# Attention: high and low query parts turned as one operand, four maxima in one narrow turn

## The chip, the cores and the metric

The kernel runs on one core of one Trainium2 chip. The metric is the device time of one launch in microseconds (us). The kernel before takes 1848.46 us, the median of three runs (1845.34 to 1849.5).

## What is computed

Two layers of a hybrid backbone over 1024 latent tokens and 128 context tokens. Each layer projects the tokens, runs a pooling mixer, softmax attention and a gated DeltaNet in parallel, gates the three and projects out. The change is in the attention alone:

```python
def one_block(qblk):
    s = jnp.einsum('bqkgd,bskd->bkgqs', qblk, k, preferred_element_type=jnp.float32) * scale
    p = jax.nn.softmax(s, axis=-1).astype(v.dtype)
    return jnp.einsum('bkgqs,bskd->bqkgd', p, v)
```

There are 8 query heads and 2 key/value heads of dimension 64. Latent queries see 1024 latent keys, 128 cached keys and their own softmax; context queries see the 128 context keys.

## The kernel before

Everything is float32 in effect. A score needs more precision than one pass of the fast format (fp32r) gives, so each operand is split into a high part (its fp32r rounding) and a low part (the rest), and a score is the sum high x high + high x low + low x high.

**How the attention is tiled.** Work goes by "pairs" p = 0 to 8. Pair 0 is the context. Pairs 1 to 8 are each one block of 512 latent tokens of one key head and one pair of its query heads. Each pair has two "asks" (p, i), i = 0 and 1, of four blocks of 128 queries, 18 asks in a layer. A pair has 9 steps (pair 0 has one), one for each tile of 128 keys: 73 steps in a layer. `BASE[p]` is the first step of pair p: 1, 10, 19, 28, 37, 46, 55, 64 for p = 1 to 8. In step n TensorE makes the scores of both query halves (L1642 and L1643, bank 0 and bank 1 of PSUM), ScalarE takes the exponential (L1492), GpSimd adds up the exponentials (L1426) and TensorE multiplies them with the values (L1652). `scores(n)` needs the exponentials of step n-1, since the two banks are used again.

**How a query gets ready.** GpSimd's `split` (L1400) writes the high part twice side by side into `qhh` (two casts, L1409) and the low part into `ql` (L1412); for the first four asks ScalarE makes the high part (`query_high`, L1501). TensorE turns the four blocks of `qhh` (item "hi", four transposes, L1559) into PSUM bank 7 and ScalarE copies them into `QH` (L1468), so that rows 0 to 63 and rows 64 to 127 of `QH` both hold the high part. Item "max" multiplies a block with all keys (L1606) and VectorE reduces it to one maximum for each query (L1679), written into column 64 of `ql`. Item "lo" turns the four blocks of `ql` with that column (four transposes of 65 columns, L1588), and ScalarE copies the 65 rows into `QL` (L1468). Row 64 of `KO` is -1, so the maximum is subtracted within the second score product.

**How keys get ready.** ScalarE and GpSimd make high and low parts in `khl` (L1498, L1431) while TensorE runs the scan of the DeltaNet. `key_turn` turns them between scan steps (L1569). ScalarE copies both into `KH` (`keys_turned`, L1507) and later the high part from `KH` into `KO` (`keys_copied`, L1512).

**What sets the order.** Each engine's instructions run in the written order. `attention_slots` (L1243) writes it: in slot n TensorE does scores(n+1), then the slot's items, then the values of step n; ScalarE does the exponentials of step n+1, then the copies of the slot's items; VectorE does the slot's items. The items of pair p with b = `BASE[p]` lie at:

```python
slots[b - 8].append(("hi", p, 1))
slots[b - 6].append(("lo", p, 0))
slots[b - 2].append(("lo", p, 1))
if p >= 3:
    slots[b - 12].append(("hi", p, 0))
```

The DeltaNet's outputs are turned as items "o" in slots 8 to 16 (L1625). Items "hi", "lo", "sum" and "o" all use PSUM bank 7, so each turn waits until the copy of the turn before it is done (`turn_start`, L1548). Asks of pairs 0 and 1 and "hi" (2, 0) come before the steps, in the list `first` (L1245). The scores of a pair's first step wait for the copy of its "lo" (p, 1) (L1637). GpSimd's adds and splits are in one order too (L1449 to L1463).

## Time and profile before

| | |
|---|---|
| median of the runs | 1848.46 us |
| the profiled execution | 1844.25 us, its span on the core 1842.6 us |
| busy TensorE / VectorE / ScalarE / GpSimd | 91% / 53% / 34% / 50% of the span |
| granted clock of TensorE, mean | 0.964 of full speed |
| attention steps, layer 1 and layer 2 | 577.5 to 803 us and 1496 to 1722 us |

PE is TensorE's matmul, PEld its weight load, DVE VectorE, ACT ScalarE, POOL GpSimd, SP the queue that issues transfers. In a timeline row the first number is the start in us from the start of the span, the second how long the row took; "x4" means four instructions merged, and then the second number runs from the first start to the last end. Behind it, in brackets, stands how long the engine was idle before it and which instruction ended that wait.

### The profile page before, as it was taken

Reading aid. Unit: us, or ns where it says so; the run is one execution under the profiler, and the core shown is the slowest. Engines: PE = TensorE matmul, PEld = TensorE weight load, DVE = VectorE, ACT = ScalarE, POOL = GpSimd, SP = SyncE. Lnnn points to the kernel's source line nnn. Section 1 sums busy time; section 2 is a strip of 40 time slices with the busy share of each in tenths; the row PEclk is TensorE's granted clock in tenths of the full one; section 3 lists DMA queues with packets and bytes.
Section 4 is the critical chain, followed back from the end, with each engine's and each line's share of the span. In section 5 each row is a group of like instructions: output and inputs, shape, how many; then the busy total and the mean of one; then the engine's idle time right before and its main releaser. Section 6 shows DMA issues by size and latency. Waiting matters only on the chain. (4 is left out here: it accounts for less than half of the span.)

```text
span 1842.6 us, 40839 instructions
## 1 busy us (share of the span) xinstructions
PE 1678.3 (91%) x17404; PEld 1367.6 (74%) x17404; DVE 978.3 (53%) x1476; ACT 623.5 (34%) x1238; POOL 928.4 (50%) x858
## 2 busy tenths in 40 slices
PE   4999999989988899979849999999899888999798
PEld 3898999979975445548728989999799754455586
DVE  2646316377736785552126563164677467955611
ACT  4322310144443444451133223111444424444511
POOL 1003395089943878832210033950899448788332
PEclk8999999999988999989969999999999999999899
DMA  9301113110000020032283011121100000200222
GB/s 338 120 14 59 61 58 93 59 37 21 4 11 13 6 58 17 12 115 92 82 308 124 31 59 61 58 85 64 39 22 4 12 13 6 64 12 12 115 91 92
DMA packets 71247, 117.22 MB, mean 64 GB/s; under 512 B 10129, under 2 KB 42129, under 8 KB 71057
## 3 DMA queue, kind: packets, MB, share of 16 engines
q1 hardware_dynamic: 70128, 114.18, 18.3%
q8 instruction: 140, 2.29, 0.5%
q10 hardware_dynamic: 928, 0.34, 0.1%
q14 instruction: 51, 0.41, 0.1%
HBM read 95.03 MB, written 19.47 MB: 62 GB/s over the span
## 5 line engine op out<-in xcount | busy, mean ns | idle before, releaser
L1426 POOL TENSOR_TENSOR attn_accp<-attn_accp,attn_pr 128x1024 f32<-128x1024 f32 x112 | 268.7, 2399 | 49.3 <-ACT attn_pr L1492 43.3
L93 PE MATMUL ps<-h_hi,in_w_hi 128*128 128x384 f32 (+1 forms) x816 | 275.9, 338 | 5.0 <-DVE h_lo L456 4.9
L94 PE MATMUL ps<-h_lo,in_w_hi 128*128 128x384 f32 (+1 forms) x816 | 274.6, 336 | 0.0
L95 PE MATMUL ps<-h_hi,in_w_lo 128*128 128x384 f32 (+1 forms) x816 | 274.4, 336 | 0.0
L1679 DVE TENSOR_REDUCE attn_ql<-ps 128x1 f32<-128x1152 f32 x128 | 172.9, 1356 | 119.9 <-PE ps L1606 119.5
L1492 ACT ACTIVATE attn_pr<-ps 128x512 f32<-128x512 f32 x292 | 158.6, 595 | 189.9 <-PE ps L1643 189.1
L93 PEld LDWEIGHTS ps<-h_hi,in_w_hi 128*128 128x128 f32 (+1 forms) x816 | 150.1, 184 | 13.1 <-issue 6.7
L94 PEld LDWEIGHTS ps<-h_lo,in_w_hi 128*128 128x128 f32 (+1 forms) x816 | 150.2, 184 | 3.9
L95 PEld LDWEIGHTS ps<-h_hi,in_w_lo 128*128 128x128 f32 (+1 forms) x816 | 150.1, 184 | 3.9
L1642 PEld LDWEIGHTS ps<-attn_QH,attn_KH 128*128 128x128 f32 x292 | 55.0, 188 | 126.3 <-issue 53.5
L1652 PE MATMUL ps<-attn_pr,z 128*64 128x512 f32 x520 | 141.3, 622 | 0.0
L908 POOL TENSOR_TENSOR delta_ML<-delta_EK,local 128x256 f32<-128x256 f32 x180 | 130.5, 746 | 14.9 <-PE ps L945 14.2
L1642 PE MATMUL ps<-attn_QH,attn_KH 128*128 128x512 f32 x292 | 131.2, 449 | 2.5 <-ACT attn_pr L1492 2.5
L945 PE MATMUL ps<-delta_TR,delta_ML 64*64 64x64 f32 x2880 | 112.8, 224 | 16.1 <-POOL delta_ML L908 10.1
L93 PE MATMUL ps<-in_w_hi,h_hi 128*128 128x256 f32 x432 | 124.6, 288 | 0.0
L288 POOL TENSOR_TENSOR in_scratch<-zz 128x1175 f32<-128x1175 f32 x4 | 9.3, 2332 | 228.0 <-ACT zz L716 228.0
L94 PE MATMUL ps<-in_w_lo,h_hi 128*128 128x256 f32 x432 | 122.9, 284 | 0.0
L95 PE MATMUL ps<-in_w_hi,h_lo 128*128 128x256 f32 x432 | 122.8, 284 | 0.0
L945 PEld LDWEIGHTS ps<-delta_TR,delta_ML 64*64 64x64 f32 x2880 | 98.9, 138 | 23.9 <-issue 11.7
L1643 PE MATMUL ps<-attn_QL,attn_KO 65*128 65x512 f32 x292 | 115.9, 397 | 0.0
L352 DVE CAST in_w_hi<-in_w 128x2048 fp32r<-128x2048 f32 (+1 forms) x24 | 31.1, 1295 | 152.7 <-DMA in_w<-in_w_in 152.7
L1606 PE MATMUL ps<-attn_KH,attn_QH 128*128 128x384 f32 x384 | 94.8, 358 | 14.3 <-DVE attn_ql L1679 13.3
(248 smaller groups left out, 3604.3 us busy)
## 6 DMA issues: line engine op xcount, KB each, us to landing
in_w<-in_w_in SPq DMA_DIRECT2D x22, 1024.0 KB, 6.0
zz<-in_w_mod SPq DMA_DIRECT2D x8, 2048.0 KB, 13.3
gates<-in_gate SPq DMA_DIRECT2D x48, 192.0 KB, 1.9
attn_gt<-gates SPq DMA_DIRECT2D x34, 256.0 KB, 2.6
z<-in_w_mod SPq DMA_DIRECT2D x4, 2048.0 KB, 10.2
out_w<-in_w_out SPq DMA_DIRECT2D x16, 512.0 KB, 7.0
delta_GB<-gc_rows SPq DMA_DIRECT2D x36, 128.0 KB, 2.9
z<-out_y SPq DMA_DIRECT2D x9, 512.0 KB, 10.7
```

Of the source, the lines that this page charges most:

```text
L93: nc.tensor.matmul(out, a_hi(i), b_hi(i), start=(i == 0), stop=False)
L94: nc.tensor.matmul(out, a_hi(i), b_lo(i), start=False, stop=False)
L95: last = nc.tensor.matmul(out, a_lo(i), b_hi(i), start=False, stop=(i == n - 1))
L908: nc.gpsimd.tensor_tensor(pairs(ML[d][:, i % 2]), EA[d][:, j % 3, :, 0], level_mask(i, d), ALU.mult).then_inc(ml_done, 1)
L945: last = nc.tensor.matmul(heads(bank, off)[rows(c), h, :], lhs(rows(c), h), rhs(rows(c), h), start=True, stop=True)
L1426: nc.gpsimd.tensor_tensor(acc, a, pr[:, n % 4], ALU.add).then_inc(pool_added, 1)
L1492: nc.scalar.activation(pr[:, n % 4, e], ps[:, e, :], ACT.Exp, scale=HD ** -0.5).then_inc(p_done, 1)
L1606: last = nc.tensor.matmul(ps[:, bank + c, 0:GRP], QH[:, p % 3, blk // 2, col:col + P], KH[:, g, GRP * c:GRP * c + GRP], start=True, stop=True)
L1642: nc.tensor.matmul(ps[:, e, :], KH[:, g, ks], QH[:, p % 3, e, :], start=True, stop=False)
L1643: nc.tensor.matmul(ps[:, e, :], KO[0:HD + 1, g, ks], QL[0:HD + 1, p % 2, e, :], start=False, stop=True).then_inc(st_done, 1)
L1652: nc.tensor.matmul(ps[HD * e:HD * e + HD, 2 + p % 2, :], values(p, kt, e), pr[:, n % 4, e], start=(kt == 0), stop=(kt == STEPS_OF[p] - 1)) ...
L1679: nc.vector.tensor_reduce(ql[:, a % 4, blk, HD:HD + 1], ps[:, bank:bank + 3, 0:GRP], AX_XY, ALU.max).then_inc(mx_read, 1)
```

## The change

The roles of the halves are exchanged. The query operand now has the high part in columns 0 to 63 and the low part in columns 64 to 127 (`qhl`), so one turn of four blocks brings both. The keys are laid out to fit: `KH` holds the high part in both row halves, `KO` the low part and four rows of -1 below it. The first score product is key high x (query high + query low), the second key low x query high, minus the maximum. ScalarE copies a turned "hi" item twice: 128 rows into `QH`, and rows 0 to 63 again into `QM`. The maxima of an ask's four blocks stand in four columns of `mx`; the "lo" item is one transpose of 4 columns, which gives 4 rows of 128. ScalarE spreads them with four small copies into rows 64 to 67 of `QM`, one for each block, each with a per-partition scale that is a unit column of the identity, so that for a block one row has its maximum and three rows are zero. For the keys, ScalarE copies the low half into `KO` and the high half into rows 64 to 127 of `KH`, and GpSimd copies that to rows 0 to 63 (`keys_doubled`). GpSimd's split has one cast in place of two, and `query_high` one activation in place of two. The copies from `KH` to `KO` are gone.

```diff
-    QL, rc = sb("QL", [P, 2, 2, QB], F32R), sb("rc", [P, 2, QB])
+    rc = sb("rc", [P, 2, QB])
+    sb("gap", [P, 1408])
-    QH = sb("QH", [P, 3, 2, QB], F32R)
-    qhh, ql = sb("qhh", [P, 4, 4, P]), sb("ql", [P, 4, 4, HD + 2])
+    QH, QM = sb("QH", [P, 3, 2, QB], F32R), sb("QM", [P, 3, 2, QB], F32R)
+    qhl, mx = sb("qhl", [P, 4, 4, P]), sb("mx", [P, 4, 4])
...
@@ GpSimd: split
-            for e in range(2 if n >= 4 else 0):
-                nc.gpsimd.tensor_copy(blocks(qhh[:, n % 4, :, HD * e:HD * e + HD], p).bitcast(F32R), q)
+            hi, lo = (blocks(qhl[:, n % 4, :, HD * e:HD * e + HD], p) for e in range(2))
             if n >= 4:
+                nc.gpsimd.tensor_copy(hi.bitcast(F32R), q)
                 pool.drain()
-            nc.gpsimd.tensor_tensor(blocks(ql[:, n % 4, :, 0:HD], p), q, blocks(qhh[:, n % 4, :, 0:HD], p),
-                                    ALU.subtract).then_inc(q_split, 1)
+            nc.gpsimd.tensor_tensor(lo, q, hi, ALU.subtract).then_inc(q_split, 1)
...
+        def keys_doubled(j):
+            pool.wait_ge(k_act, j + 1)
+            cols = slice(256 * j, 256 * j + 256)
+            pool.drain()
+            nc.gpsimd.tensor_copy(KH[0:HD, :, cols], KH[HD:P, :, cols]).then_inc(k_both, 1)
+            pool.drain()
...
         split(0, 0)
+        keys_doubled(0)
+        keys_doubled(1)
         split(0, 1)
         key_low(4)
+        keys_doubled(2)
         split(1, 0)
+        keys_doubled(3)
         split(1, 1)
-        pool.drain()
-        nc.gpsimd.memset(KO[HD:HD + 1].bitcast(F32), -1.0).then_inc(ones_done, 1)
+        keys_doubled(4)
+        nc.gpsimd.memset(KO[HD:HD + 4].bitcast(F32), -1.0).then_inc(ones_done, 1)
...
@@ ScalarE: evict
-                copied(item, query_columns(QH[:, p % 3], p, i), turned_columns(slice(0, P), p))
+                is_turned(act, *item)
+                nc.scalar.activation(query_columns(QH[:, p % 3], p, i), turned_columns(slice(0, P), p), ACT.Copy)
+                nc.scalar.activation(query_columns(QM[0:HD, p % 3], p, i), turned_columns(slice(0, HD), p),
+                                     ACT.Copy).then_inc(turn_copied, 1)
...
-                r = slice(0, HD + 1)
-                copied(item, query_columns(QL[r, p % 2], p, i), turned_columns(r, p))
+                is_turned(act, *item)
+                for b in range(4):
+                    e, c = (i, P * b) if p == 0 else (b // 2, 256 * i + P * (b % 2))
+                    last = nc.scalar.activation(QM[HD:HD + 4, p % 3, e, c:c + P], ps[0:4, 7, 0:P], ACT.Copy, scale=m["ident"][0:4, b:b + 1])
+                last.then_inc(turn_copied, 1)
...
@@ ScalarE: keys_turned; keys_copied and its calls are removed
-            nc.scalar.activation(KH[:, :, 256 * j:256 * j + 256], ps[:, K_BANKS[j], :].rearrange("p (g c) -> p g c", g=2),
-                                 ACT.Copy).then_inc(k_act, 1)
+            lo, hi = (ps[HD * e:HD * e + HD, K_BANKS[j], :].rearrange("p (g c) -> p g c", g=2) for e in range(2))
+            cols = slice(256 * j, 256 * j + 256)
+            nc.scalar.activation(KO[0:HD, :, cols], lo, ACT.Copy)
+            nc.scalar.activation(KH[HD:P, :, cols], hi, ACT.Copy).then_inc(k_act, 1)
...
@@ TensorE: the "lo" item, the first maxima and the scores
-                for blk in range(4):
-                    last = nc.tensor.transpose(ps[0:HD + 1, 7, P * blk:P * blk + P], ql[:, n % 4, blk, 0:HD + 1], m["ident"])
-                last.then_inc(turned, 1)
+                nc.tensor.transpose(ps[0:4, 7, 0:P], mx[:, n % 4, :], m["ident"]).then_inc(turned, 1)
...
                     pe.wait_ge(o_out, NT)
+                    pe.wait_ge(k_both, len(K_BANKS))
...
-                nc.tensor.matmul(ps[:, e, :], KO[0:HD + 1, g, ks], QL[0:HD + 1, p % 2, e, :],
+                nc.tensor.matmul(ps[:, e, :], KO[0:HD + 4, g, ks], QM[0:HD + 4, p % 3, e, :],
...
@@ VectorE: maximum
-                nc.vector.tensor_reduce(ql[:, a % 4, :, HD], ps[:, bank, :].rearrange("p (h c) -> p h c", c=P), AX_X,
+                nc.vector.tensor_reduce(mx[:, a % 4, :], ps[:, bank, :].rearrange("p (h c) -> p h c", c=P), AX_X,
```

## Rows read from the trace of the kernel before

**Rows 1.** Windows: busy us (xinstructions) by engine, clock, DMA, first layer's steps
```profile
577.50:803.00 225.50, 211.26 (x910) 112.05 (x910) 148.51 (x129) 103.87 (x192) 176.72 (x102) 0.99 0.07 19
```

**Rows 2.** Groups by line, shapes apart: busy us, mean ns | idle before
```profile
L1588 PE MATMUL ps<-masks,attn_ql 128*65 128x128 f32 x144 | 23.4, 288 | 3.4 <-DVE attn_ql L1679 3.1 <-ACT attn_QL L1468 0.3
...
L1468 ACT ACTIVATE attn_QL<-ps 65x512 fp32r<-65x512 f32 x36 | 21.4, 594 | 43.7 <-PE ps L1588 43.7
...
L714 ACT ACTIVATE zz<-ps 128x384 f32<-128x384 f32 x32 | 14.8, 491 | 67.0 <-PE ps L95 67.0
...
L1144 ACT ACTIVATE pbr<-ps,cols 128x384 f32<-128x384 f32 x12 | 6.5, 576 | 4.3 <-PE ps L1059 2.6 <-PE ps L1062 1.7
...
L716 ACT ACTIVATE zz<-ps 128x128 f32<-128x128 f32 x16 | 4.4, 275 | 0.0
...
L1409 POOL CAST attn_qhh<-z 128x256 fp32r<-128x256 f32 x56 | 21.9, 417 | 10.2 <-PE ps L1588 10.2
```

**Rows 3.** Timeline, a "lo" turn, the values behind it, the next exponentials
```profile
596.14 0.60 PE L1588 MATMUL ps<-masks,attn_ql 128*65 128x128 f32 x4
596.67 1.08 PE L1652 MATMUL ps<-attn_pr,z 128*64 128x512 f32 x4
...
598.45 1.09 ACT L1492 ACTIVATE attn_pr<-ps 128x512 f32<-128x512 f32 x2 [1.07 <-PE ps L1643]
```

**Rows 4.** Timeline around slot 17, the first scores of pair 3
```profile
641.01 1.09 ACT L1492 ACTIVATE attn_pr<-ps 128x512 f32<-128x512 f32 x2 [1.19 <-PE ps L1643]
...
642.43 0.59 ACT L1468 ACTIVATE attn_QL<-ps 65x512 fp32r<-65x512 f32 x1 [0.34 <-PE ps L1588]
...
643.33 0.50 PE L1642 MATMUL ps<-attn_QH,attn_KH 128*128 128x512 f32 x1
```

**Rows 5.** Timeline around slot 62, the first scores of pair 8
```profile
776.37 0.59 ACT L1468 ACTIVATE attn_QL<-ps 65x512 fp32r<-65x512 f32 x1
...
777.21 0.50 PE L1642 MATMUL ps<-attn_QH,attn_KH 128*128 128x512 f32 x1
```

**Rows 6.** Timeline in slot 8, a "lo" turn with an "o" turn behind it
```profile
609.47 0.59 ACT L1468 ACTIVATE attn_QL<-ps 65x512 fp32r<-65x512 f32 x1 [0.36 <-PE ps L1588]
...
610.11 0.44 PE L1625 MATMUL ps<-masks,of 128*128 128x128 f32 x2 [0.68 <-ACT attn_QL L1468]
```

**Rows 7.** Timeline of TensorE, "hi" (3, 0) in slot 7
```profile
605.68 0.63 PE L1559 MATMUL ps<-masks,attn_qhh 128*128 128x128 f32 x4 [1.44 <-POOL attn_ql L1412]
```

**Rows 8.** Timeline of the stage ahead of the steps, first layer
```profile
570.63 4.12 DVE L1679 TENSOR_REDUCE attn_ql<-ps 128x1 f32<-128x1152 f32 x3 [0.39 <-PE ps L1606]
...
575.55 0.59 ACT L1468 ACTIVATE attn_QL<-ps 65x512 fp32r<-65x512 f32 x1 [2.10 <-PE ps L1588]
...
576.30 0.60 PE L1559 MATMUL ps<-masks,attn_qhh 128*128 128x128 f32 x4
...
578.16 0.47 PE L1642 MATMUL ps<-attn_QH,attn_KH 128*128 128x512 f32 x1 [1.26 <-ACT attn_pr L1492]
```

**Rows 9.** Timeline of the last key turn, in the scan, and the first maxima
```profile
544.10 0.60 ACT L1509 ACTIVATE attn_KH<-ps 128x512 fp32r<-128x512 f32 x1 [0.60 <-PE ps L1569]
...
544.80 0.30 ACT L1498 ACTIVATE attn_khl<-z 128x128 fp32r<-128x128 f32 x1
...
545.17 0.45 POOL L1431 TENSOR_TENSOR attn_khl<-attn_ck,attn_khl 128x128 f32<-128x128 f32 x1 [1.46 <-ACT attn_khl L1498]
...
546.09 0.66 PE L1569 MATMUL ps<-masks,attn_khl 128*128 128x128 f32 x4 [1.41 <-POOL attn_khl L1431]
...
560.69 1.08 PE L1601 MATMUL ps<-attn_KH,attn_QH 128*128 128x128 f32 x8 [0.62 <-DVE of L1215]
```

**Rows 10.** Timeline of TensorE, from a wide stationary operand to one of 16 columns
```profile
136.91 0.34 PE L95 MATMUL ps<-h_hi,in_w_lo 128*128 128x384 f32 x1
137.08 0.34 PE L93 MATMUL ps<-h_hi,in_w_hi 128*16 128x384 f32 x1
```

**Rows 11.** Timeline of TensorE, the values of step 0
```profile
582.58 1.98 PE L1652 MATMUL ps<-attn_pr,z 128*64 128x512 f32 x4
```

More of the change, by code:

```diff
@@ L1291, in attention @@
     khl = sb("khl", [P, KT_CTX + 1, NKV, P])
-    QH = sb("QH", [P, 3, 2, QB], F32R)
-    qhh, ql = sb("qhh", [P, 4, 4, P]), sb("ql", [P, 4, 4, HD + 2])
+    QH, QM = sb("QH", [P, 3, 2, QB], F32R), sb("QM", [P, 3, 2, QB], F32R)
+    qhl, mx = sb("qhl", [P, 4, 4, P]), sb("mx", [P, 4, 4])
     onc = sb("onc", [P, 1])
     cache_in, on_in, kv_out = sem("cache_in"), sem("on_in"), sem("kv_out")
-    ones_done, k_high, k_split, k_turned, k_act, k_copied, q_high = (
-        sem(n) for n in ("ones_done", "k_high", "k_split", "k_turned", "k_act", "k_copied", "q_high"))
+    ones_done, k_high, k_split, k_turned, k_act, k_both, q_high = (
+        sem(n) for n in ("ones_done", "k_high", "k_split", "k_turned", "k_act", "k_both", "q_high"))
     turned, turn_copied = sem("turned"), sem("turn_copied")
@@ L1497, in key_high @@
             for ks, k in keys_of(j):
-                last = nc.scalar.activation(khl[:, ks, :, 0:HD].bitcast(F32R), k, ACT.Copy)
+                last = nc.scalar.activation(khl[:, ks, :, HD:P].bitcast(F32R), k, ACT.Copy)
             last.then_inc(k_high, 1)
@@ L1502, in query_high @@
             n = ASKS.index((p, i))
-            for e in range(2):
-                last = nc.scalar.activation(blocks(qhh[:, n % 4, :, HD * e:HD * e + HD], p).bitcast(F32R), queries(p, i), ACT.Copy)
-            last.then_inc(q_high, 1)
+            nc.scalar.activation(blocks(qhl[:, n % 4, :, 0:HD], p).bitcast(F32R), queries(p, i), ACT.Copy).then_inc(q_high, 1)
         def keys_turned(j):
             act.wait_ge(k_turned, j + 1)
-            nc.scalar.activation(KH[:, :, 256 * j:256 * j + 256], ps[:, K_BANKS[j], :].rearrange("p (g c) -> p g c", g=2),
-                                 ACT.Copy).then_inc(k_act, 1)
-        def keys_copied(j):
-            act.wait_ge(k_act, j + 1)
-            nc.scalar.activation(KO[0:HD, :, 256 * j:256 * j + 256], KH[0:HD, :, 256 * j:256 * j + 256],
-                                 ACT.Copy).then_inc(k_copied, 1)
+            lo, hi = (ps[HD * e:HD * e + HD, K_BANKS[j], :].rearrange("p (g c) -> p g c", g=2) for e in range(2))
+            cols = slice(256 * j, 256 * j + 256)
+            nc.scalar.activation(KO[0:HD, :, cols], lo, ACT.Copy)
+            nc.scalar.activation(KH[HD:P, :, cols], hi, ACT.Copy).then_inc(k_act, 1)
         for j in range(4):
@@ L1530, in scalar @@
         evict(("hi", 0, 1))
-        for j in range(3):
-            keys_copied(j)
         evict(("hi", 1, 0))
-        for j in range(3, 5):
-            keys_copied(j)
         act.wait_ge(on_in, 32)
@@ L1558, in query_turn @@
         for blk in range(4):
-            last = nc.tensor.transpose(ps[:, 7, P * blk:P * blk + P], qhh[:, n % 4, blk, :], m["ident"])
+            last = nc.tensor.transpose(ps[:, 7, P * blk:P * blk + P], qhl[:, n % 4, blk, :], m["ident"])
         last.then_inc(turned, 1)
@@ L1634, in scores @@
                 pe.wait_ge(ones_done, 1)
-                pe.wait_ge(k_copied, len(K_BANKS))
             if kt == 0:
```

4 lines of the change are left out of this document (2 added, 2 removed).

## The prediction

> **What bounds the kernel now.** I read the page first. Its chain of work that ended last lies in the output projection and says nothing of the attention, so I went to the windows. In the first layer's steps (225.5 us) TensorE is busy for 211.26 us at a clock of 0.99, GpSimd for 176.72, VectorE for 148.51, ScalarE for 103.87 [rows 1]. The second layer's window reads alike. So the steps are bound by TensorE, and TensorE's own list of waits says where not. Then the timelines, slot by slot. The reader is to see three things there: the transposes that the change removes are short and overlap [rows 2, 3], the copy behind a "lo" turn has room in most slots but none in some [rows 4 to 6], and ahead of the steps TensorE is not the bound, VectorE's reductions and ScalarE's copies are [rows 8].
>
> **What a turn costs.** Four transposes take 0.60 us from the first start to the last end [rows 3] and one about 0.27 (the mean of 0.288 over 144 [rows 2] holds some at half the clock). So one follows another by (0.60 - 0.27) / 3 = 0.11 us, and three fewer free 0.33 us of TensorE. There are 36 "lo" turns in the two layers: at most 36 x 0.33 = 11.9 us. That is the whole prize, and each turn has to be asked who waits for what behind it. I take the one transpose of 4 columns at the time of one of 65: a stationary operand of 16 columns follows one of 128 after 0.17 us, the spacing of its neighbours, with no gap [rows 10].
>
> **What spreading costs.** One copy of 65x512 took 0.59 us [rows 2]. Four copies of 4x128 from PSUM with a scale read from SBUF replace it. The trace has a 128x128 copy from PSUM at 0.275, and the price of such a scale by 128x384 with and without: 0.576 - 0.491 = 0.085 [rows 2]. That makes 0.36 for one. Two exponentials of 0.595 take 1.09 together [rows 4], so each starts 0.10 before the end of the one ahead; the four take 0.36 + 3 x 0.26 = about 1.16 us. The low bound is 3 x 0.20 + 0.27 = 0.87, by the spacing of the two small key casts (the one at 544.80 came 0.20 after its neighbour) and no price for the scale [rows 9, 2]. The high bound is no overlap, 4 x 0.365 = 1.46. I take 1.16, since the shape and the scale are both priced by near rows.
>
> For this term the Trainium skill (ScalarE: Activation LUTs, section What ACT_TABLE_LOAD costs) gives 186 ns plus 0.833 ns a column, 93 ns more for a pointer operand, and an overlap of 93 ns: an estimate of 0.386 + 3 x 0.293 = 1.27 us for the four. By that figure the sum below would end some 1.9 us later (0.105 us at nine places in each layer). It agrees with the rows within a tenth and speaks against the change, since most of a small copy is its fixed part.
>
> **The "lo" turns of a layer, all 18.**
> - (4, 0) to (8, 0), in slots b - 6: nothing waits for the copy soon. The turn would end at 596.14 + 0.27 = 596.41 and the next exponentials move from 598.45 to 598.12 [rows 3]; 1.16 fits. Each frees 0.33: 5 x -0.33 = -1.65.
> - (3, 1) to (7, 1), in slots b - 2: the pair's first scores wait for the copy. Before, it started at 642.43 and was over 0.3 before the scores at 643.33 [rows 4]. Now the turn ends 0.33 earlier, ScalarE is just free of the exponentials (641.01 + 1.09 = 642.10), and the copies end at 642.10 + 1.16 = 643.26; with 0.06 for the signal the scores start at 643.32. TensorE would be ready at 643.00. The gain is eaten whole: 5 x 0.
> - (8, 1), slot 62, has no "max" item ahead of it, so ScalarE, not the turn, sets the start: 776.37 as before, end 777.53, scores at 777.59 in place of 777.21 [rows 5]: +0.38.
> - (2, 1) and (3, 0), slots 8 and 13: an "o" turn waits in the same slot for the bank. The copy starts at 609.47 - 0.33 = 609.14 and ends at 610.30, the "o" turn comes at 610.35 in place of 610.11 [rows 6]: 2 x +0.24 = +0.48.
> - (2, 0), slot 4: "hi" (3, 0) waits 1.44 us for GpSimd three slots later [rows 7] and swallows it: 0.
> - (0, 0): ahead of the steps, at half the clock, it held up the next maximum's product, and VectorE stood idle for 0.39 [rows 8]. I take most of that: -0.35.
> - (0, 1) and (1, 0): under VectorE's reductions, three in 4.12 us without a gap [rows 8]: 0.
> - (1, 1): next point.
>
> **The start of the steps.** Before, VectorE ends at 570.63 + 4.12 = 574.75, the "lo" (1, 1) turn follows, its copy starts at 575.55, "hi" (2, 0) is turned at 576.30 and copied, and only then come the exponentials of step 0, for which the scores of step 1 wait till 578.16 [rows 8]. Now the copies run from 575.22 to 576.38, the turn comes at 576.44 (+0.14), and its second copy puts another 0.49 (the spacing of two copies of 512 columns [rows 4]) ahead of the exponentials: +0.63.
>
> **The second copy of a "hi" item** adds 0.49 us on ScalarE 36 times. In most slots ScalarE has 1 us to spare. In slots 11 and 16 an "o" turn waits for it as the one of slot 8 does for its "lo" [rows 6]: 2 x +0.49 = +0.98.
>
> **GpSimd's split** loses one cast (0.42 by its mean [rows 2], and a little of it overlaps its neighbour, so I take 0.35), and "hi" (3, 0) comes that much earlier [rows 7]: -0.35. Elsewhere the splits are early.
>
> **The keys.** ScalarE's copy of each turned key tile becomes two, 0.49 more. The first three hide beside scan steps. The fourth, at 544.10, is in front of the casts of the last key tile, GpSimd's 0.9 us after them and the turn that TensorE already waits 1.41 us for, with scan steps queued behind it [rows 9]: 546.09 becomes 546.58, +0.49. The five doublings on GpSimd are of 64x512; by the cast of 128x256 at about 0.4 they take some 0.65 each. The maxima first need `k_both` at 560.69 [rows 9]. Even if all five only began when the last key turn is over, at 546.6 + 0.7, and the last two splits and the memset lay between them, they would be done with microseconds in hand: hidden. The five copies to `KO` that go, and the halved `query_high`, were beside scan steps: 0. Were the cover gone, the five would cost 3.3 us a layer.
>
> **The sum for a layer:** -1.65 + 0.38 + 0.48 - 0.35 + 0.63 + 0.98 - 0.35 + 0.49 = +0.61; two layers +1.2 us. Against the profiled execution (1844.25 us, span 1842.6) that is 1845.5; that execution lies 4.2 below the median, and on the median of 1848.46 the forecast is 1849.7. With four copies in 0.87 us the places read: slots b - 2 five times -0.30, slot 62 +0.09, slots 8 and 13 -0.05 each, start +0.34; sum -2.05 a layer, -4.1 in all. With 1.46 us: five times +0.29, +0.68, twice +0.54, start +0.93; +3.26 a layer, +6.5 in all.
>
> **The rivals.** A difference under 0.2% (3.7 us) cannot be told from none in this kernel.
> - Small copies are quicker than I price them, so that TensorE's gain comes through at the pair starts: 1848.5 - 4.1 = 1844.4. For it: only 4 of 128 partitions are written, and the small casts lay 0.20 apart [rows 9]. Against it: the scale's 0.085 [rows 2]. It decides from about 0.9 us for the four. Chance 0.23.
> - The other side, ScalarE becomes the bound at the pair starts: the four don't overlap. 1848.5 + 6.5 = 1855.0. Place: slots b - 2; it decides from about 1.35 us for the four. For it: the scale is one more read at each start. Against it: the exponentials overlap by 0.10 [rows 4]. Chance 0.15.
> - A narrow turn makes TensorE drain. From the last transpose's start to the half-width values there are 596.67 - (596.14 + 3 x 0.11) = 0.20 us where 0.11 is the spacing [rows 3]: 0.1 us for the change of shape. Once more at 13 turns a layer (five freed, five at pair starts, slots 8 and 13, (1, 1)) it would be +2.6 us: 1852.3. Against it rows 10. Chance 0.05. The Trainium skill (TensorEngine Tiling (Array Packing), Key Properties) says that changing the tiling mode drains TensorE; whether 4 columns are another mode no row here shows.
> - The clock falls longer at the start. Behind the wait of 1.26 us [rows 8] the values of step 0 took 1.98 us [rows 11], where later ones take 1.08 [rows 3]: half the clock. With 0.6 us more waiting ahead of them another step's worth might go, about 1.4 us a layer, 1852.5. Chance 0.07.
> - That the copies hide wholly and all 11.9 us come is excluded by rows 5 and 6.
>
> **How the numbers follow.** The forecast has 0.47, and its own range is 1846.5 to 1852.5. The range of 1843.5 to 1856 takes in the first two rivals and about 1 us beyond them. Faster: nearly all of the first rival and a tail, 0.25. Slower: most of the second, part of the two small ones and a tail, 0.26. The rest, 0.49, is no difference.
>
> **What would show it.** Each "lo" item is one transpose of about 0.27 us with the values 0.20 us behind its start; four ScalarE copies in 1.16 us; the first scores of pairs 3 to 7 wait about 0.3 us for them; "o" turns in slots 8, 11, 13, 16 wait 1.1 to 1.3 us in place of 0.7; the last key turn waits 0.5 us longer; `k_both` ends nobody's wait. The prediction is wrong if the four copies take under 0.9 or over 1.35 us, if TensorE has a gap around the narrow turn, or if VectorE's and GpSimd's order shifts so that TensorE's waits for them grow or go.

## The result, and the profile after

The changed kernel takes 1864.64 us, the median of five runs (1859.85 to 1868.04). The kernel before, run beside it, takes 1847.26 (1845.34 to 1849.5, five runs). The ratio is 1.0092, with a 95% interval of 1.007 to 1.0114. So the change costs about 17 us, where 1.2 were forecast. The profiled execution took 1868.04 us, its span is 1866.3. From the two pages, the busy times (before, then after) and the granted clock after in 40 slices:

```profile
PE 1678.3 (91%) x17404; PEld 1367.6 (74%) x17404; DVE 978.3 (53%) x1476; ACT 623.5 (34%) x1238; POOL 928.4 (50%) x858
```

```profile
PE 1691.6 (91%) x17296; PEld 1368.1 (73%) x17296; DVE 977.0 (52%) x1476; ACT 657.8 (35%) x1374; POOL 923.9 (50%) x840
...
PEclk8999999999987999989869999999999879999899
```

The engines' shares hardly differ from those of before. But TensorE carries 108 instructions fewer and is busy 13.3 us longer, and its mean clock is 0.947, where it was 0.964. So the time has to be looked for by stage. I cut each layer at three instructions of TensorE that both kernels have: the first product of the DeltaNet scan, the first "max" product, and the first product that sums the exponentials (item "sum"), up to the last of these. The windows of the kernel before, first layer (us, then busy us by PE, PEld, DVE, ACT and POOL, the granted clock, the DMA share, GB/s):

```profile
535.40:560.70 25.30, 22.54 (x597) 19.35 (x597) 12.25 (x43) 11.90 (x28) 8.77 (x12) 0.90 0.07 18
560.70:586.40 25.70, 19.34 (x79) 13.43 (x79) 14.67 (x12) 5.95 (x11) 6.90 (x7) 0.80 0.07 22
586.40:802.10 215.70, 204.02 (x889) 108.39 (x889) 145.80 (x127) 100.67 (x185) 176.72 (x102) 1.00 0.07 20
```

The same windows of the changed kernel, first layer; the second layer's read alike, with clocks of 0.85, 0.59 and 0.98:

```profile
532.60:560.60 28.00, 23.98 (x596) 20.55 (x597) 12.35 (x43) 13.23 (x28) 11.77 (x17) 0.84 0.07 16
560.60:589.80 29.20, 22.27 (x67) 14.59 (x67) 14.50 (x12) 8.68 (x24) 6.26 (x5) 0.59 0.06 19
589.80:807.40 217.60, 202.53 (x847) 104.05 (x847) 145.53 (x127) 114.11 (x240) 172.38 (x90) 0.98 0.07 20
```

| us, layer 1 and layer 2 | before | after | difference |
|---|---|---|---|
| scan | 25.3, 23.2 | 28.0, 27.5 | +2.7, +4.3 |
| start: first maximum to first sum | 25.7, 25.1 | 29.2, 29.2 | +3.5, +4.1 |
| steps: first to last sum | 215.7, 215.8 | 217.6, 217.7 | +1.9, +1.9 |

The six differences add up to 18.4 us. The two profiled executions lie further apart than the medians (spans of 1866.3 and 1842.6 us, 23.7 apart, against 17.4), and the other 5.3 us lie in stages that no kernel here changes. The longest of these, between the steps of layer 1 and the scan of layer 2, takes 654.4 us before and 660.9 after, and 654.2 to 661.2 over all the profiles of this document. So a single stage of one profile proves little, and the ratios decide.

The clock is the first thing to see. In the start of layer 1 TensorE carries 12 instructions fewer and is busy for 2.93 us longer (22.27 against 19.34), at a granted clock of 0.59 in place of 0.80. In the steps it is not so: TensorE is busy 1.49 us less and the stage is still 1.9 longer.

**The keys.** Timelines of TensorE and ScalarE in the scan of the changed kernel, first layer:

```profile
540.67 0.65 PE L1577 MATMUL ps<-masks,attn_khl 128*128 128x128 f32 x4
...
541.85 0.59 ACT L1526 ACTIVATE attn_KO<-ps 64x512 fp32r<-64x512 f32 x1
542.45 0.59 ACT L1527 ACTIVATE attn_KH<-ps 64x512 fp32r<-64x512 f32 x1
543.07 0.31 ACT L1515 ACTIVATE attn_khl<-attn_ck 128x128 fp32r<-128x128 f32 x1
...
544.57 1.03 PE L1577 MATMUL ps<-masks,attn_khl 128*128 128x128 f32 x4 [2.63 <-POOL attn_khl L1431]
545.53 0.69 PE L1079 MATMUL ps<-delta_S,zz 64*64 64x64 f32 x8
...
548.45 0.45 PE L1079 MATMUL ps<-delta_S,zz 64*64 64x64 f32 x8
```

These answer to [rows 9]. The wait ahead of the last key turn is 2.63 us, where it was 1.41. Behind it the turn takes 1.03 us (0.66 before) and eight scan products 0.69 us, where the same eight take 0.45 three microseconds later: TensorE runs at 1.2 GHz (granted clock 0.50) from the end of the wait to about 548.1, some 3.4 us. Before, the turn and the products behind it ran at 2.4 GHz.

**The start of the steps**, which answers to [rows 8]:

```profile
574.95 0.27 PE L1595 MATMUL ps<-masks,attn_mx 128*4 128x128 f32 x1 [1.81 <-DVE attn_mx L1685]
575.25 1.10 ACT L1493 ACTIVATE attn_QM<-ps,masks 4x128 fp32r<-4x128 f32 x4 [1.56 <-PE ps L1595]
575.96 0.63 PE L1648 MATMUL ps<-attn_QH,attn_KH 128*128 128x512 f32 x1
576.81 1.05 PE L1567 MATMUL ps<-masks,attn_qhl 128*128 128x128 f32 x4
...
579.60 0.76 PE L1648 MATMUL ps<-attn_QH,attn_KH 128*128 128x512 f32 x1 [1.74 <-ACT attn_pr L1509]
...
585.44 1.98 PE L1658 MATMUL ps<-attn_pr,z 128*64 128x512 f32 x4
```

**Slot 7**, which answers to [rows 7]:

```profile
608.77 0.63 PE L1567 MATMUL ps<-masks,attn_qhl 128*128 128x128 f32 x4 [1.42 <-POOL attn_qhl L1413]
609.33 1.79 PE L1658 MATMUL ps<-attn_pr,z 128*64 128x512 f32 x4
...
613.47 0.27 PE L1595 MATMUL ps<-masks,attn_mx 128*4 128x128 f32 x1
614.94 0.44 PE L1632 MATMUL ps<-masks,of 128*128 128x128 f32 x2 [1.20 <-ACT attn_QM L1493]
```

The wait is 1.42 us, as it was 1.44 [rows 7], and yet the values behind it take 1.79 us. In the kernel before they took 1.08:

```profile
606.24 1.08 PE L1652 MATMUL ps<-attn_pr,z 128*64 128x512 f32 x4
...
608.83 0.60 PE L1588 MATMUL ps<-masks,attn_ql 128*65 128x128 f32 x4
```

From the values to the "lo" turn it is 613.47 - 609.33 = 4.14 us, before 608.83 - 606.24 = 2.59: 1.55 us lost to the clock alone, and 1.55 in the second layer too.

That the wait is as long as before hides that both its sides came earlier. GpSimd's casts, before and after:

```profile
603.94 0.73 POOL L1409 CAST attn_qhh<-z 128x256 fp32r<-128x256 f32 x2
```

```profile
607.37 0.39 POOL L1411 CAST attn_qhl<-z 128x256 fp32r<-128x256 f32 x1
```

The low part starts 0.87 us behind the first cast before (604.81) and 0.53 after (607.90). TensorE is there sooner by the 0.33 of the narrow turn in slot 4. From the first sum to this turn it is 608.77 - 589.78 = 18.99 us, before 605.68 - 586.36 = 19.32.

The changed kernel's steps have a second stretch of 3.4 us at half the clock in each layer, at 684.3 us in the first, behind a wait for VectorE. After, and the same place before:

```profile
684.70 1.30 PE L1613 MATMUL ps<-attn_KH,attn_QH 128*128 128x384 f32 x3 [1.63 <-DVE attn_mx L1685]
```

```profile
679.59 0.77 PE L1606 MATMUL ps<-attn_KH,attn_QH 128*128 128x384 f32 x3 [1.32 <-DVE attn_ql L1679]
```

From there to the next scores it is 688.41 - 684.70 = 3.71 us, before 681.74 - 679.59 = 2.15: another 1.56. The kernel before has no such stretch in the steps of either layer.

**What was done to the steps themselves.** The groups of the new operations (busy us, mean ns, idle time of the engine before them):

```profile
L1493 ACT ACTIVATE attn_QM<-ps,masks 4x128 fp32r<-4x128 f32 x144 | 39.7, 344 | 31.4 <-PE ps L1595 30.6
L1486 ACT ACTIVATE attn_QM<-ps 64x512 fp32r<-64x512 f32 x36 | 21.0, 582 | 0.0
...
L1595 PE MATMUL ps<-masks,attn_mx 128*4 128x128 f32 x36 | 10.3, 285 | 4.3 <-DVE attn_mx L1685 3.6 <-ACT attn_QM L1493 0.4
```

Pair 3's start (slot 17) answers to [rows 4], pair 8's (slot 62) to [rows 5]:

```profile
647.59 0.27 PE L1595 MATMUL ps<-masks,attn_mx 128*4 128x128 f32 x1
647.80 1.08 PE L1658 MATMUL ps<-attn_pr,z 128*64 128x512 f32 x4
647.90 1.10 ACT L1493 ACTIVATE attn_QM<-ps,masks 4x128 fp32r<-4x128 f32 x4
649.06 0.50 PE L1648 MATMUL ps<-attn_QH,attn_KH 128*128 128x512 f32 x1 [0.19 <-ACT attn_QM L1493]
...
782.52 0.50 PE L1648 MATMUL ps<-attn_QH,attn_KH 128*128 128x512 f32 x1 [0.72 <-ACT attn_QM L1493]
```

TensorE's waits in the steps, first layer, after (total us, times, longest):

```profile
PE ps L1632 <- ACT attn_QM L1493: 2.4, 2, 1.2
PE ps L1632 <- ACT attn_QM L1486: 2.4, 2, 1.2
PE ps L1648 <- ACT attn_QM L1493: 1.7, 6, 0.7
```

and before:

```profile
PE ps L1625 <- ACT attn_QH L1468: 1.4, 2, 0.8
PE ps L1625 <- ACT attn_QL L1468: 1.4, 2, 0.7
```

The "o" turns (L1632, before L1625) wait 4.8 us for ScalarE's copies where they waited 2.8, and the pairs' first scores (L1648) wait 1.7 us in all. That is the new waiting of the steps, of the size that was forecast.

### The profile page after: what moved, and what is told of

Read it like the earlier page. It is cut to its first block and busy times, and to the rows that moved or that the text cites. A ratio compares the mean times of both kernels' runs of the same rounds, so it can differ in the third digit from the quotient of the medians.

```text
span 1866.3 us, 40759 instructions
## 1 busy us (share of the span) xinstructions
PE 1691.6 (91%) x17296; PEld 1368.1 (73%) x17296; DVE 977.0 (52%) x1476; ACT 657.8 (35%) x1374; POOL 923.9 (50%) x840
## 5 line engine op out<-in xcount | busy, mean ns | idle before, releaser
L1685 DVE TENSOR_REDUCE attn_mx<-ps 128x1 f32<-128x1152 f32 x128 | 172.9, 1356 | 130.8 <-PE ps L1613 130.0
L1648 PEld LDWEIGHTS ps<-attn_QH,attn_KH 128*128 128x128 f32 x292 | 56.7, 194 | 134.8 <-issue 56.3
L1648 PE MATMUL ps<-attn_QH,attn_KH 128*128 128x512 f32 x292 | 134.7, 461 | 6.9 <-ACT attn_pr L1509 3.5
L288 POOL TENSOR_TENSOR in_scratch<-zz 128x1175 f32<-128x1175 f32 x4 | 10.2, 2555 | 228.1 <-ACT zz L716 228.1
L1649 PE MATMUL ps<-attn_QM,attn_KO 68*128 68x512 f32 x292 | 119.8, 410 | 0.0
L945 PEld LDWEIGHTS ps<-delta_TR,delta_ML 64*64 64x64 f32 x2880 | 98.7, 138 | 23.4 <-DVE delta_TR L1186 11.1
L1613 PE MATMUL ps<-attn_KH,attn_QH 128*128 128x384 f32 x384 | 99.7, 374 | 12.4 <-DVE attn_mx L1685 11.2
L352 DVE CAST in_w_hi<-in_w 128x2048 fp32r<-128x2048 f32 (+1 forms) x24 | 27.5, 1147 | 152.3 <-DMA in_w<-in_w_in 152.3
## 6 DMA issues: line engine op xcount, KB each, us to landing
zz<-in_w_mod SPq DMA_DIRECT2D x8, 2048.0 KB, 13.3
```

The lines of the kernel that those rows point to most:

```text
L945: last = nc.tensor.matmul(heads(bank, off)[rows(c), h, :], lhs(rows(c), h), rhs(rows(c), h), start=True, stop=True)
L1613: last = nc.tensor.matmul(ps[:, bank + c, 0:GRP], QH[:, p % 3, blk // 2, col:col + P], KH[:, g, GRP * c:GRP * c + GRP], start=True, stop=True)
L1648: nc.tensor.matmul(ps[:, e, :], KH[:, g, ks], QH[:, p % 3, e, :], start=True, stop=False)
L1649: nc.tensor.matmul(ps[:, e, :], KO[0:HD + 4, g, ks], QM[0:HD + 4, p % 3, e, :], start=False, stop=True).then_inc(st_done, 1)
L1685: nc.vector.tensor_reduce(mx[:, a % 4, blk:blk + 1], ps[:, bank:bank + 3, 0:GRP], AX_XY, ALU.max).then_inc(mx_read, 1)
```

## The experiments

**The theory after the result:** the change's own operations cost about what was forecast. The loss is TensorE's clock: one wait that grew in the scan (ahead of the last key turn) and the wait ahead of the scores of step 1 are followed by stretches at half the clock. **The rivals:** the added work itself (ScalarE's second copies, the spread copies) is the loss; or the narrow transpose costs TensorE more than its record shows. Each kernel was timed in five rounds against the kernel before.

**1. The last key tile goes first** (changed kernel; ScalarE's casts of it move ahead of the turned tiles 1 to 3, GpSimd's low part ahead of the second doubling).

```diff
@@ GpSimd
         keys_doubled(0)
+        key_low(4)
         keys_doubled(1)
         split(0, 1)
-        key_low(4)
@@ ScalarE
         keys_turned(0)
+        key_high(4)
...
         keys_turned(3)
-        key_high(4)
```

> The changed kernel with the casts of the last key tile moved ahead: on ScalarE they come right after the first turned key tile, on GpSimd the low part right after the first doubling. That takes away TensorE's wait of 2.63 us ahead of the last key turn. Two theories. Waits alone: what a wait costs is its own length; the kernel gains what the wait was, about 2.6 us a layer, 5.2 in all, 1859.4. Clock: behind the wait TensorE also works for some 3.4 us at the lower of its two clock levels (1.2 GHz), which costs about 1.7 us more a layer; the gain is about 8.6 us, 1856.0, and the scan stage takes about 23.5 us in both layers at a granted clock near 0.95, where it took 28.0 and 27.8 at 0.84.

Measured: 1857.06 us, ratio 1.003 (1.001 to 1.0051), where the changed kernel stands at 1.0092. The scan and the start in the first layer:

```profile
535.40:558.80 23.40, 20.44 (x597) 17.40 (x597) 11.97 (x43) 13.33 (x28) 11.81 (x17) 1.00 0.08 20
558.80:588.00 29.20, 22.27 (x67) 14.57 (x67) 14.50 (x12) 8.73 (x24) 6.23 (x5) 0.59 0.06 19
```

The scan falls from 28.0 to 23.4 us (second layer 27.5 to 24.9) with the same work on every engine. The long wait is gone (0.42 us in place of 2.63), and no stretch at half the clock follows it in either layer. Not all of it is the edit's doing: in the changed kernel a stretch at half the clock, begun ahead of the scan, runs 5.3 us into layer 1's scan, and here there is none. The start of layer 1 stays at 29.2 and 0.59. The ratio falls by 0.62%, about 11 us, which the two intervals leave open by some 6 us to either side; the two scans show 7.2 of it. So the order of one key tile carries a good part of the loss, and a second place is left.

**2. Long fillers in five waits of the changed kernel, and 3. in the kernel before.** Products whose result nobody reads, ahead of the wait for the last key turn, "lo" (1, 1), the scores of step 1, the second maximum of step 0, and "hi" (3, 0): 5, 4, 4, 3, 3 of them in the changed kernel and 3, 3, 2, 3, 3 in the one before.

```diff
+    def fillers(pe, bank, count):
+        for _ in range(count):
+            nc.tensor.matmul(ps[:, bank, :], m["ident"], m["masks"][:, 0:4, :].rearrange("p a c -> p (a c)"), start=True, stop=True)
...
+                if (p, i) == (1, 1):
+                    fillers(pe, 7, 4)
```

> The changed kernel with idle time of TensorE filled by products that nobody reads (128x512 float32, about 0.43 us each): five ahead of the last key turn, four ahead of the lo (1, 1) turn, four ahead of the scores of step 1, three ahead of the second maximum of pair 2, three ahead of hi (3, 0). No wait is taken away; each is only worked through. Waits alone: no gain, perhaps 1 us lost, 1864 to 1866. Clock: the stretches at half the clock behind those waits go, about 1.7 us at the scan, 2 to 3 at the start and 1.7 in slot 7 of each layer; the gain is 8 to 12 us, 1853 to 1857, and the granted clock of the start stage rises from 0.59 to over 0.85.

> The kernel before with the same fillers at the same places (three, three, two, three, three). Waits alone: no gain, 1847 to 1848. Clock: it has one stretch at half the clock at the start of the steps in each layer and a slow first part of the maxima; 1.5 to 3 us a layer come back, 1842 to 1844.

Measured: 1866.05 us, ratio 1.0084 (1.0061 to 1.0107), and 1857.72, ratio 1.0049 (1.0031 to 1.0068). Both missed what the clock theory had expected (1853 to 1857, and 1842 to 1844). The clock did come back: from the "lo" (1, 1) turn to the first sum neither kernel stands at half the clock at all, and the start of the changed kernel's second layer has 0.94 in place of 0.59. The time did not, because my fillers were too long:

```profile
1480.86 4.56 PE L1558 MATMUL ps<-masks 128*128 128x512 f32 x10
```

Five of them (two records each) took 4.56 us where the wait was 2.65, so they held TensorE up themselves.

**4. The kernel before, with its key copy split in two** (64x512 twice in place of 128x512, and nothing else).

```diff
-            nc.scalar.activation(KH[:, :, 256 * j:256 * j + 256], ps[:, K_BANKS[j], :].rearrange("p (g c) -> p g c", g=2),
-                                 ACT.Copy).then_inc(k_act, 1)
+            nc.scalar.activation(KH[0:HD, :, cols], lo, ACT.Copy)
+            nc.scalar.activation(KH[HD:P, :, cols], hi, ACT.Copy).then_inc(k_act, 1)
```

> The kernel before with one part of the change alone: the copy of a turned key tile is split in two copies of 64x512, from rows 0 to 63 and from rows 64 to 127. Output unchanged. The first theory of the prediction: the wait ahead of the last key turn grows by 0.49, +1 us in all. Waits alone with the spacing seen after (0.60 from copy to copy, no overlap): the wait grows by 1.2, +2.4 us, 1849.7. Clock: the longer wait is followed by half the clock as well, +3 us a layer, +6 in all, 1853.

Measured: 1857.75 us, ratio 1.0045 (1.0028 to 1.0062). The scan takes 26.9 and 27.2 us. TensorE:

```profile
544.72 0.66 PE L1571 MATMUL ps<-masks,attn_khl 128*128 128x128 f32 x4 [2.96 <-POOL attn_khl L1431]
...
547.19 1.12 PE L1561 MATMUL ps<-masks,attn_qhh 128*128 128x128 f32 x4
```

One split copy, which adds 0.6 us to ScalarE five times a layer, costs the kernel before 8 us (0.45%). The wait is 2.96 us in place of 1.41, and the next turn ("hi", not the key turn itself) takes 1.12 in place of 0.66. TensorE stands at half the clock behind the wait for 3.4 us in layer 1 and 5.8 in layer 2, before for none. So this part of the change makes the longer wait and the slow stretch by itself.

**5. Short fillers** (changed kernel, the same five places and counts 5, 4, 4, 3, 3, but 256 columns).

```diff
-            nc.tensor.matmul(ps[:, bank, :], m["ident"], m["masks"][:, 0:4, :].rearrange("p a c -> p (a c)"), start=True, stop=True)
+            nc.tensor.matmul(ps[:, bank, 0:256], m["ident"], m["masks"][:, 0:2, :].rearrange("p a c -> p (a c)"), start=True, stop=True)
```

> The changed kernel with fillers of half the width. The fillers before took 0.85 us each, not 0.43 (eight records in 3.60 us for four), so they were longer than the waits that they were to fill, and what the clock gave back they took. Now 128x256, about 0.43 us each, five ahead of the last key turn and four, four, three, three at the start and in slot 7. Waits alone: 1864 to 1866 beside a kernel before of about 1850, ratio 1.008 to 1.009. Clock: the scan stage falls from 28 to about 26, the stage from the first maxima to the first sum from 29.2 to about 26, slot 7's half-clock stretch goes; 5 to 7 us a layer, ratio 1.002 to 1.004.

Measured: 1852.87 us, ratio 1.0005 (0.9984 to 1.0026). The start of the first layer, window and timeline:

```profile
560.90:585.40 24.50, 20.44 (x89) 14.14 (x89) 14.40 (x12) 8.47 (x24) 6.25 (x5) 0.93 0.07 23
```

```profile
573.10 1.99 PE L1558 MATMUL ps<-masks 128*128 128x256 f32 x8 [0.61 <-ACT attn_QM L1493]
...
575.51 0.40 PE L1662 MATMUL ps<-attn_QH,attn_KH 128*128 128x512 f32 x1
...
582.68 1.08 PE L1672 MATMUL ps<-attn_pr,z 128*64 128x512 f32 x4
```

This kernel does everything the changed one does and 19 useless products a layer more, and its ratio is 0.87% lower. The start takes 24.5 us at a clock of 0.93 in place of 29.2 at 0.59; a score product takes 0.40 us in place of 0.63, the values of step 0 1.08 in place of 1.98. TensorE's busy time falls by 1.8 us although it has 22 instructions more. In the second layer the start takes 25.4 us at 0.80. That rules out the first rival for most of the loss: with all copies in place it goes.

**6. The second copy of a "hi" item on VectorE** (from `QH` into `QM`, so that ScalarE is rid of it).

```diff
-                nc.scalar.activation(query_columns(QM[0:HD, p % 3], p, i), turned_columns(slice(0, HD), p),
-                                     ACT.Copy).then_inc(turn_copied, 1)
...
+                nc.vector.tensor_copy(query_columns(QM[0:HD, p % 3], p, i), query_columns(QH[0:HD, p % 3], p, i)).then_inc(q_both, 1)
```

> The changed kernel with ScalarE's second copy of a hi item (PSUM to QM, 64x512) replaced by a VectorE copy from QH, behind the signal for the turn. Waits alone: the o turns in slots 11 and 16 wait 0.7 in place of 1.2, the exponentials of step 0 come 0.5 earlier: about 1.5 us a layer, 3 in all. Clock: the same, and less of the half-clock stretch ahead of the first values (1.74 us of waiting becomes about 1.3): 3 to 5 us a layer at the start if the stretch shrinks to what the kernel before has.

Measured: 1878.49 us, ratio 1.0137 (1.0108 to 1.0166), a miss. The reason is the casts' price (group by line), and that four of them stand ahead of the first maxima (timeline of VectorE and GpSimd):

```profile
L1695 DVE CAST attn_QM<-attn_QH 64x512 fp32r<-64x512 f32 x36 | 45.6, 1279 | 10.4 <-ACT attn_QH L1485 10.4
```

```profile
563.24 5.24 DVE L1695 CAST attn_QM<-attn_QH 64x512 fp32r<-64x512 f32 x4
563.40 4.13 POOL L1458 TENSOR_TENSOR attn_osq<-of 128x2304 f32<-128x2304 f32 x1 [7.08 <-DVE of L1215]
```

Four took 5.24 us; 3 to 5 us a layer had been expected as a gain. The quickest of the 36 casts took 0.353 us and the longest 4.242, about as long as GpSimd's one product of 4.13 beside it: it looks as if VectorE stood still while GpSimd worked. The start takes 33.2 us. The Trainium skill (SBUF — State Buffer, SBUF: two separate sides) says that VectorE in some modes and GpSimd share a pair of ports by an exclusive lock, and that the loser blocks for the whole instruction; these rows agree with it. That run says nothing on what ScalarE's second copy costs; it only shows that VectorE is no home for it.

**7. Four narrow turns in place of one** (the same transpose four times, so that the turn is as long as before).

```diff
-                nc.tensor.transpose(ps[0:4, 7, 0:P], mx[:, n % 4, :], m["ident"]).then_inc(turned, 1)
+                for blk in range(4):
+                    last = nc.tensor.transpose(ps[0:4, 7, 0:P], mx[:, n % 4, :], m["ident"])
+                last.then_inc(turned, 1)
```

> The changed kernel with its one narrow transpose done four times over, into the same place, so the number of transposes is that of the kernel before. It prices the prize of the change. By the prediction 0.33 us comes back only at the five free turns of a layer, slots 8 and 13 and the start: 0.33 x 8 x 2 = about 5 us longer than the changed kernel at most, 3.3 by the five alone. If narrow transposes are cheaper than wide ones (0.27 us in both by the rows, spacing unknown) it is less. If the ScalarE copies had hidden all of it everywhere: 0.

Measured: 1874.56 us, ratio 1.0125 (1.0093 to 1.0157), 0.33% or 6 us above the changed kernel's 1.0092; the two intervals overlap. The steps take 219.9 and 222.6 us where they took 217.6 and 217.7. TensorE:

```profile
599.06 0.60 PE L1596 MATMUL ps<-masks,attn_mx 128*4 128x128 f32 x4
599.59 1.08 PE L1660 MATMUL ps<-attn_pr,z 128*64 128x512 f32 x4
```

Four narrow transposes take 0.60 us, as four of 65 columns did [rows 3], with the values 0.53 behind their start; one takes 0.27 with the values 0.21 behind. So narrow operands take the same time as wide ones, there is no gap around them, and the second rival falls. What the narrow turn gives can only be estimated: about 6 us by the ratios, which their intervals don't set apart from nothing, and 2.3 and 4.9 us by the steps of one profile, where 3.3 to 5 had been expected in all and 11.9 were the most it could give. In slot 7 this kernel's wait is 1.10 us, and no half clock follows it in either layer.

**8. The kernel before with the last key tile first; 9. and 10. both kernels with both mends** (last key first, and short fillers at the four places that are left: 4, 4, 3, 3 in the changed kernel, 3, 2, 3, 3 in the one before). The edits are those of 1 and 5.

```diff
@@ the kernel before, ScalarE
+        key_high(4)
...
         keys_turned(3)
-        key_high(4)
```

> The kernel before with the last key tile's casts moved ahead, on both engines. Takes away its wait of 1.41 us ahead of the last key turn. Waits alone: 1.4 us a layer, 2.8 in all, ratio 0.9985. Clock: no half-clock stretch follows that wait in the kernel before, so the same 2.8.

> The changed kernel with the last key tile's casts first (no wait to fill at the scan) and the short fillers at the start and in slot 7. The two mends act on different stages: scan 28 to about 24 and first maxima to first sum 29 to about 25 in each layer. Both hold by the clock theory: about 8 us a layer against the changed kernel, ratio to the kernel before 0.996 to 1.001. If they share a cause and don't add up, it stays at the 1.0005 of the short fillers or 1.003 of the casts alone.

> The kernel before with the same two mends (fillers three, two, three, three, of 128x256). By the clock theory it has less to give back: one half-clock stretch at the start of each layer, and 1.4 us of wait at the scan. Ratio 0.994 to 0.998. If the change's own products are worth anything once the clock is kept, the changed and mended kernel (sent with this one) is faster than this one; by the prediction's ledger without start and keys (-1.65 + 0.38 + 0.48 + 0.98 - 0.35 = -0.16 a layer) the two differ by under 1 us in the steps.

| kernel | us | ratio (interval) | scan | start | steps |
|---|---|---|---|---|---|
| 8, before, key first | 1851.73 | 0.9982 (0.996 to 1.0004) | 24.3, 24.3 | 27.4, 26.1 | 216.3, 215.9 |
| 9, changed, both mends | 1846.97 | 0.9986 (0.9968 to 1.0004) | 25.3, 25.6 | 24.9, 27.6 | 216.5, 215.0 |
| 10, before, both mends | 1843.45 | 0.9961 (0.9939 to 0.9983) | 24.1, 22.2 | 24.7, 24.7 | 215.6, 215.6 |

(The kernel before, run beside kernels 8 to 11, itself stood at 1849.7 to 1852.9; the ratios are what compares.) With both mends the changed kernel stands at the kernel before or just under it: the whole 0.92% is got back. But the same mends help the kernel before as well, and it stays 0.25% ahead, with overlapping intervals. Both ratios have the same kernel before in them; the 12 executions of each kernel, set against each other, have means of 1847.1 and 1842.3 us, 4.9 apart with a standard error of 1.4 if the executions are independent. So the changed kernel is very likely still the slower one, by a few microseconds. Kernel 8 gained about what its 1.4 us of wait a layer were worth, with an interval that takes in nothing. Kernel 10 is 0.39% under the kernel before, clear of its interval.

**11. Kernel 9 with the turns of a pair one slot earlier**, so that the pair's first scores don't wait for the spread copies.

```diff
-        slots[b - 2].append(("lo", p, 1))
+        slots[b - 2 if p == 2 else b - 3].append(("lo", p, 1))
-            slots[b - 12].append(("hi", p, 0))
+            slots[b - 12 if p == 3 else b - 13].append(("hi", p, 0))
```

> The changed and mended kernel with the lo (p, 1) turn one slot earlier from pair 3 on, and hi (p, 0) one slot earlier from pair 4 on to make room. It takes the spreading copies off the path at the pair starts. By the prediction the gain of 0.33 us at (3, 1) to (7, 1) was eaten by the copies and 0.38 were lost at (8, 1): 5 x 0.33 + 0.38 + 0.33 = 2.4 us a layer come back, 4.7 in all, if the stage of the steps (217.6 us from first to last sum) falls to about 215.2.

Measured: 1848.89 us, ratio 0.9999 (0.9978 to 1.0019), so not quicker than kernel 9. The waits of the first scores are gone, but one came up elsewhere, since all these items share bank 7:

```profile
639.32 0.44 PE L1642 MATMUL ps<-masks,of 128*128 128x128 f32 x2 [1.72 <-ACT attn_QM L1493]
```

The steps take 216.3 us in both layers; kernel 9 has 216.5 and 215.0.

**Where the clock stood.** The granted clock, read in windows of half a microsecond, gives how long TensorE stood at 1.2 GHz in each part of layer 1 and layer 2 (us, one profile of each kernel):

| kernel | scan up to the last key turn | from there to the first maximum | first maximum to "lo" (1, 1) | from there to the first sum | steps |
|---|---|---|---|---|---|
| before | 5.2, 0.0 | 0.0, 0.0 | 6.8, 3.4 | 3.4, 3.4 | 0.0, 0.0 |
| changed | 5.3, 5.0 | 3.4, 3.2 | 10.2, 10.2 | 13.7, 13.7 | 6.8, 6.8 |
| 1 | 0.0, 3.4 | 0.0, 0.0 | 10.2, 7.5 | 13.6, 13.0 | 6.8, 3.4 |
| 4 | 0.0, 1.0 | 3.4, 5.8 | 10.2, 6.8 | 3.4, 6.8 | 2.2, 1.3 |
| 5 | 0.0, 4.9 | 0.0, 0.0 | 3.4, 10.2 | 0.0, 0.0 | 3.4, 0.0 |
| 9 | 5.3, 5.3 | 0.0, 0.0 | 6.8, 16.9 | 0.0, 0.2 | 3.4, 0.1 |
| 10 | 5.2, 0.0 | 0.0, 0.0 | 10.2, 10.2 | 0.0, 0.0 | 3.4, 3.4 |

Two columns follow the experiments. Behind the last key turn there is a slow stretch in all eight layers that waited 2.63 to 2.96 us there (the changed kernel, 4, 6 and 7) and in none of the other 18. From "lo" (1, 1) to the first sum there is none, but for 0.2 us, in the twelve layers with fillers (2, 3, 5, 9, 10 and 11), 3.4 to 6.8 us in the kernel before, 4 and 8, and 6.8 to 13.7 in the unfilled changed kernels. The first and the third column don't follow them: the kernel before has 5.2 us in one layer's scan and none in the other's, with the same instructions. So about 2 us of the 4.3 by which the second layer's scan grew are no effect of the key wait (up to the last key turn it took 11.84 us after 8.64, and the wait had grown by 1.23), and it is there that kernels 9 and 10 differ most, in their second layers.

## Why the prediction was wrong

The forecast, +1.2 us, was right about most of the change's own operations, wrong about the keys and above all about the clock. By its own steps:

- **The price of spreading** (1.16 us, bounds 0.87 and 1.46) was right: 1.10 (0.36 + 3 x 0.26 is 1.14, not 1.16, which changes nothing). The Trainium skill's figure gave an estimate of 1.27 (ScalarE: Activation LUTs, What ACT_TABLE_LOAD costs); one copy took 0.344 against its 0.386, so that figure is a little high here.
- **The first two rivals** fall with it. 1.10 us lies between their points of decision, 0.9 and 1.35.
- **Pair starts (0)**: right. The first scores wait 0.19 us in slot 17 and 1.7 us in all six places, 0.3 expected. From turn to scores it is 649.06 - 647.59 = 1.47 us, before 643.33 - 641.79 = 1.54; the gain is eaten.
- **Slot 62 (+0.38)**: right. From turn to scores it is 782.52 - 780.52 = 2.00 us; before 777.21 - 775.67 = 1.54, so +0.46.
- **"o" turns in slots 8, 13, 11 and 16 (+0.48 and +0.98)**: the sum of four waits went from 2.8 to 4.8, +2.0 where 1.46 was forecast.
- **A narrow turn drains TensorE**: no. The values start 0.21 us behind its start, 0.20 expected without a drain, and four of them take what four wide ones took. What the Trainium skill says on a drain between tiling modes (TensorEngine Tiling (Array Packing), Key Properties) doesn't show for operands of 4 columns.
- **The split (-0.35)** came, though the wait of slot 7 looks untouched (1.42 us after 1.44). Both sides of the wait moved by a third of a microsecond, as the rows of slot 7 show; the narrow turn of slot 4, which I had swallowed by this wait, is TensorE's side.
- **(0, 0), ahead of the steps (-0.35)** is hidden in the changed kernel: from the first maximum to the end of VectorE's reductions it is 574.80 - 560.61 = 14.19 us, before 574.75 - 560.69 = 14.06. The idle time of 0.39 ahead of the last reductions is gone, but TensorE stood at half the clock for 10.2 us there and not for 6.8, and VectorE's idle time ahead of the first large reduction is 0.95 in place of 0.41. Kernel 9, with 6.8 us at half the clock as before, takes 571.48 - 557.90 = 13.58.
- **The start of the steps (+0.63)**: the second copy did add its 0.48 (the wait ahead of step 1's scores is 1.74 us, it was 1.26). But from the end of VectorE's reductions to the values of step 0 it is 585.44 - 574.80 = 10.64 us, before 582.58 - 574.75 = 7.83: +2.8. The rest is the same work at half the clock: "hi" (2, 0) takes 1.05 in place of 0.60, the first score product 0.76 in place of 0.47.
- **The doublings** were hidden: the last ends at 551.49, 9 us ahead of the first maximum at 560.61.
- **The keys (+0.49)**: the first step that failed. I said that the first three copies hide beside scan steps. They don't. ScalarE's work lies end to end from 538.97 us on, with the copies of turned keys 0.60 apart and not 0.49, and all of it stands ahead of the last tile's casts. These start 543.07 - 541.32 = 1.75 us after the fourth tile's turn is over; before, the same turn ended at 544.07 and they started at 544.60, 0.53 behind. That is the 1.22 us by which the wait grew, where I had 0.49. And its cost was more than its length: behind the last key turn the scan took another 1.4 and 1.1 us longer, at half the clock. Experiments 1 and 4 show both, one by taking the wait away and one by making it alone.
- **The clock at the start**: the step that failed most. It was a rival, priced at 1.4 us a layer with a chance of 0.07, and only for the start. The start grew by 3.5 and 4.1 us, and the scan and two places in the steps belong to it too. Together with the keys it is most of the 17 us: short fillers alone brought the ratio from 1.0092 to 1.0005, and against a kernel before with the same mends 0.25% is left. I had used the clock in one place, for one step's worth of values, and had taken every duration of the start from rows at whatever clock they stood, as if it were a property of the stage.

The steps are where the ledger can be checked. Its terms there sum to -0.16 us a layer (-1.65, +0.38, +0.48, +0.98, -0.35). Measured was +1.9, with two stretches at half the clock in each layer, worth 1.55 and 1.56 us, where the kernel before has none. The changed kernel's steps go by their number: with two they take 217.6 and 217.7 us (217.6 in kernel 1), with one 216.3 to 216.5 (kernels 1, 5 and 9), with none 214.8 and 215.0 (kernels 5 and 9, whose fillers in slot 7 lie within its wait). The kernel before takes 215.7 and 215.8 with none. So at one clock the change is worth about -0.8 us a layer in the steps, and the ledger was right to within 1 us; that its sign is right is less sure, since kernel 10 has 215.6 twice, with one stretch in each.

**What stays open.** What decides whether the clock falls isn't settled. The wait in slot 7 is 1.42 us with the changed kernel and 1.44 before, with nearly the same instructions behind it, and only the one is followed by 1.2 GHz. In the second layer of kernel 1 the same wait is 1.41 and isn't followed by it. In kernel 5 the second layer's scan still takes 27.3 us at 0.91 while the wait is filled, for its first 4.9 us stand at half the clock. Nor is it shown which of the start's waits matters: the fillers went in together. Short fillers alone were never put into the kernel before. And what makes the few microseconds between kernels 9 and 10 isn't shown; in their profiles they lie in the scans and in the start of layer 2, at the slow stretches that no mend is about.

## What to carry to other kernels

Where the profile shows TensorE at half the clock behind its longest waits, an edit that makes such a wait longer can cost a multiple of what it adds to the wait, so a ledger of durations that ends near zero can lose 1%; look for these waits outside the stage that the edit is about as well, above all behind copies that you count as hidden. Before a change is credited or given up, mend the wait in both kernels: an earlier place for the one late producer, or cheap products ahead of the wait that are no longer than it, gave more here than the change did (0.39% in the kernel before).
